# Output columns 1024 to 2047 of w_out as a second panel of seven products

## What is computed

```python
merged = sigmoid(g_a) * (o_a @ w_branch_a) + sigmoid(g_b) * (o_b @ w_branch_b)
h = h + merged @ w_out
hn = rms_norm(h, norm_ffn_g)
h = h + (silu(hn @ w_ffn_gate) * (hn @ w_ffn_up)) @ w_ffn_down
```

## Time and profile before

| | |
|---|---|
| median of the runs | 1259.84 us |
| the profiled execution | 1259.98 us |
| its span | 1258.2 us |
| TensorE busy | 1253.8 us |
| VectorE busy | 1051.5 us |
| ScalarE busy | 757.4 us |
| DMA, mean | 227 GB/s |

### The profile page before, as it was taken

How to read it: one execution, slowest core, us unless ns; L and a number is a source line. 1 busy time by engine, 2 the same in 40 slices (tenths; PEclk the granted TensorE clock), 3 DMA queues, 4 the chain that set the end, 5 groups by cost and what they waited for, 6 DMA issues and landing times.

```text
span 1258.2 us, 14986 instructions
## 1 busy us (share of the span) xinstructions
PE 1253.8 (100%) x5870; PEld 1039.4 (83%) x5870; DVE 1051.5 (84%) x930; ACT 757.4 (60%) x765; POOL 92.1 (7%) x89
## 2 busy tenths in 40 slices
PE   9999999999999999999999999999999999999999
PEld 8888888888878888888888888888888888888887
DVE  6988887677889788779989888878898887888996
ACT  6766665566667555456656665556566555655653
POOL 3312312000000000000000000100000001000000
DMA  9976683855357586955777768976686679866874
GB/s 353 319 253 189 208 262 119 267 162 160 113 190 249 168 296 215 335 166 194 247 247 234 253 184 248 282 249 221 201 263 242 199 216 305 258 221 193 275 220 115
DMA packets 136933, 285.98 MB, mean 227 GB/s; under 512 B 5264, under 2 KB 11936, under 8 KB 133280
## 3 DMA queue, kind: packets, MB, share of 16 engines
q1 hardware_dynamic: 129904, 252.23, 57.0%
q0 software_dynamic: 6784, 32.53, 13.8%
q10 hardware_dynamic: 176, 0.26, 0.1%
HBM read 251.43 MB, written 8.41 MB: 207 GB/s over the span
## 4 chain that ended last, share of the span: by engine, by line
PE 99%; DMA 0%; DVE 0%; SPq 0%; ACT 0%; issue 0%
PE bank L2361 27%; PE bank L2366 27%; PE bank L2362 27%; PE bank L2304 4%; PE bank L2312 4%; PE bank L2305 4%; PE bank L2243 1%; PE bank L2256 1%; PE bank L2517 1%; PE bank L2272 1%; PE bank L2225 0%; DMA raw<-in_w_in 0%; PE bank L2274 0%; PE bank L2530 0%; PE bank L2215 0%; DVE w_lo L1544 0%
## 5 line engine op out<-in xcount | busy, mean ns | idle before, releaser
L1806 DVE TENSOR_TENSOR u_lo<-quad,u_hi 128x2048 fp32r<-128x2048 f32 x245 | 556.5, 2287 | 109.5 <-ACT u_hi L1233 60.1
L1233 ACT ACTIVATE u_hi<-quad 128x2048 fp32r<-128x2048 f32 x250 | 475.4, 1915 | 282.6 <-PE bank L2366 160.9
L2361 PE MATMUL bank<-u_hi,xT_hi 128*128 128x512 f32 x676 | 263.3, 389 | 0.0
L2362 PE MATMUL bank<-u_hi,xT_lo 128*128 128x512 f32 x676 | 263.0, 389 | 0.0
L2366 PE MATMUL bank<-u_lo,xT_hi 128*128 128x512 f32 x740 | 198.1, 389 | 0.0
L2366 PEld LDWEIGHTS bank<-u_lo,xT_hi 128*128 128x128 f32 x740 | 138.7, 188 | 29.2 <-DVE u_lo L1806 0.5
L2362 PEld LDWEIGHTS bank<-u_hi,xT_lo 128*128 128x128 f32 x676 | 126.9, 188 | 26.2
L2361 PEld LDWEIGHTS bank<-u_hi,xT_hi 128*128 128x128 f32 x676 | 126.9, 188 | 26.2
L1544 DVE TENSOR_TENSOR w_lo<-raw,w_hi 128x1024 fp32r<-128x1024 f32 (+1 forms) x64 | 73.3, 1155 | 33.7 <-ACT w_hi L1039 32.1
L2362 PE MATMUL bank<-u_hi,fT_lo 128*128 128x512 f32 (+1 forms) x236 | 90.7, 385 | 0.0
L2361 PE MATMUL bank<-u_hi,fT_hi 128*128 128x512 f32 (+1 forms) x236 | 90.7, 385 | 0.0
(11 more groups left out here) (271 smaller groups left out, 1852.0 us busy)
## 6 DMA issues: line engine op xcount, KB each, us to landing
quad<-in_w_ffn_gate SPq DMA_DIRECT2D x44, 1024.0 KB, 6.8
quad<-in_w_ffn_up SPq DMA_DIRECT2D x44, 1024.0 KB, 6.0
quad<-in_w_ffn_down SPq DMA_DIRECT2D x44, 1024.0 KB, 6.2
quad<-in_w_in SPq DMA_DIRECT2D x41, 1024.0 KB, 6.8
quad<-quad POOLq DMA_DIRECT2D x24, 1024.0 KB, 8.4
raw<-in_w_in SPq DMA_DIRECT2D x16, 1024.0 KB, 5.7
quad<-in_w_out SPq DMA_DIRECT2D x16, 1024.0 KB, 5.2
raw<-in_w_branch_b SPq DMA_DIRECT2D x8, 1024.0 KB, 9.3
```

The costliest lines, as they stand in the source:

```text
L1233: A(st.hi[u.hi][:], st.quad[slot][:], ACT.Copy).then_inc(hi_ready, u.step)
L1806: V.tensor_tensor(st.lo[u.lo][:], st.quad[u.panel.slot[u.raw]][:], st.hi[u.hi][:].bitcast(F32), ALU.subtract).then_inc(lo_ready, u.step)
L2361: M(sums, a_hi(k), hi[:, w], start=start and k == 0, stop=False, skip_group_check=True)
L2362: M(sums, a_lo(k), hi[:, w], start=False, stop=False, skip_group_check=True)
```

## The change

Columns 1024 to 2047 of w_out become a second panel `outs[1]` in the order `ORDER`; U and O units are gone. Units N2 and N3 of a w_out panel are placed in the panel behind it. `panels[0]` has the order `FFN_FIRST_ORDER`. The early units are M1 and M5 of `outs[0]`; the P of `outs[0]` is made by POOL's accumulating DMA, and Z of `outs[0]` is moved from behind N1 to behind M2. The additions to h are single (one half, one token block), and steps of h are placed anew between the units. The load of x goes out one load earlier in SP's queue and still waits for the last merge. (Core of the diff; removed runs of lines, which stand above, are left out.)

```diff
-H_AFTER = 6
-OUT_ORDER = ("M1", "U0", "M5", "M6", "M2", "M7", "N0", "M3", "N1", "M4", "N2", "N3", "U1", "U2", "U3")
+H_AFTER = 5
+OUT_ORDER = ("M1", "M5", "M6", "M2", "M7", "N0", "M3", "N1", "M4")
+FFN_FIRST_ORDER = ("M1", "N2-", "M5", "N3-", "M6", "M2", "M7", "N0", "M3", "M4", "N1")
 FIRST_ORDER = ("O0", "O1", "M1", "O2", "M5", "O3", "M6", "M2", "M7", "N0", "M3", "N1", "M4")
 ORDER = ("M1", "N2-", "M5", "N3-", "M6", "M2", "M7", "N0", "M3", "N1", "M4")
...
+def plan_outs(kt, n, first_index):
+    panels = []
+    index = first_index
+    for col, names in enumerate((OUT_ORDER, ORDER)):
+        p = Panel(n + col, "out2", col, kt, panels[-1] if panels else None)
+        p.i = -1
+        p.add_products()
+        panels.append(p)
+        for name in names:
+            u = (p.prev if name[-1] == "-" else p).unit[name[0:2]]
+            u.index = index
+            p.order.append(u)
+            index += 1
+    return panels
...
+    early = [outs[0].unit["M1"], outs[0].unit["M5"]]
...
+        out_stage = Stage(quad, quad_landed, f_stage.hi, f_stage.lo, ms_hi, ms_lo, m21[:])
+        for panel in outs:
+            panel.stage = out_stage
...
+            steps = 3 * panel.n + {"P": 1, "R": 2, "Z": 3}[name]
+            return steps - (panel.n >= outs[0].n)
+        def p_ready(panel):
+            return (p_summed, 16) if panel is outs[0] else (sum_ready, sums(panel, "P"))
...
+            def sum_p(panel):
+                st = panel.stage
+                pool.wait_ge(st.landed[panel.slot["12"]], panel.landed["12"])
+                pool.wait_ge(early_lo_ready, 1)
+                pool.dma_start(st.quad[panel.slot["11"]][:], st.quad[panel.slot["12"]][:],
+                               accum_op=ALU.add).then_inc(p_summed, 16)
...
-            sum_q(outs)
+            sum_p(outs[0])
+            sum_q(outs[0])
+            sum_q(outs[1])
...
-                    if j in jobs[-3:-1] and k == 3:
-                        early_unit_hi(jobs[-3:-1].index(j))
+                    if (j, k) in ((jobs[-3], 3), (last_bb, 2)):
+                        early_unit_hi(j is last_bb)
...
+            def outs_unit(panel, u):
+                if u.name == "M6" and panel is outs[1]:
+                    copy_m1(panel)
                 if u.name == "M7":
-                    copy_m5(outs)
+                    copy_m5(panel)
                 if u not in early:
                     unit_hi(u)
...
+                if u.name == "M6" and panel is outs[0]:
+                    copy_m1(panel)
+                if panel is outs[0]:
+                    if u.name == "N0":
+                        turned_to_hi(last_bb, mT_hi, last_bb.n)
+                else:
+                    if u.name == "N2":
+                        squares_of(0)
+                    if u.name == "M2":
+                        scaled_to_hi(0)
+                        A(x21, by_group(staged[:, 1, :]), ACT.Copy).then_inc(x21_ready, 1)
+                    if u.name == "M3":
+                        squares_of(1)
+                    if u.name == "M4":
+                        scaled_to_hi(1)
+            def first_unit(panel, u):
                 if u.name == "M6":
                     copy_m1(panel)
                 if u.name == "M7":
                     copy_m5(panel)
                 unit_hi(u)
-                if u.name == "O0":
-                    squares_of(1)
-                if u.name == "O1":
-                    scaled_to_hi(1)
-                if u.name == "M1":
+                if u.name == "N2":
                     x_forms_of_h()
                     squares_of(NB - 2)
-                if u.name == "M6":
+                if u.name == "M2":
                     scaled_to_hi(NB - 2)
-                if u.name == "N0":
+                if u.name == "M3":
                     squares_of(NB - 1)
-                if u.name == "M3":
+                if u.name == "N1":
                     scaled_to_hi(NB - 1)
...
+            def add_to_h(panel, half, t):
+                n = 2 * panel.col + half
+                sums = ((a_bank, b_bank), (c_bank, e_bank))[half][t](panel)
+                if t:
+                    dve.wait_ge(piece_used, (panel.b_done, panel.c_done)[half] + 1)
+                else:
+                    dve.wait_ge((a_summed, c_summed)[half], rows_before(panel) + 1)
+                V.tensor_tensor(h[:, t, columns_of(n)], sums[:], h[:, t, columns_of(n)],
+                                ALU.add).then_inc((h_top_ready, h_ready)[t], 1)
...
-                    if j in jobs[-3:-1] and k == 3:
-                        early_unit_lo(jobs[-3:-1].index(j))
+                    if j in (jobs[-3], last_bb) and k == 3:
+                        early_unit_lo(j is last_bb)
                     if j.prev is not None:
                         follow(j.prev, k, j.pieces)
-                    if j is last_bb and k == 3:
-                        sum_p(outs)
                     a = att_step(j, k, SPLIT_SLOTS - 1)
...
+            def outs_unit(panel, u):
+                before = panel.prev
+                if panel is outs[0]:
+                    if u.name == "M7":
+                        seed_c(panel)
+                    if u.name == "M3":
+                        seed_e(panel)
+                    if u not in early:
+                        unit_lo(u)
+                    if u.name == "M5":
+                        sum_r(panel)
+                        gate_bb(last_bb)
+                    if u.name == "M2":
+                        sum_z(panel)
+                    if u.name == "M7":
+                        merge(last_bb)
+                    if u.name == "M3":
+                        turned_to_lo(mT_hi, mT_lo, last_bb.n, last_bb.n, mT_ready)
+                else:
+                    if u.name == "M1":
+                        dve.wait_ge(h_landed, 16)
+                        add_to_h(before, 0, 0)
+                    if u.name == "M7":
+                        seed_c(panel)
                     unit_lo(u)
...
+                    if u.name == "N2":
+                        add_to_h(before, 0, 1)
+                        sum_p(panel)
+                    if u.name == "N3":
+                        sum_r(panel)
+                        scale_h(0, H_SETS + 1)
+                    if u.name == "M2":
+                        sum_z(panel)
+                    if u.name == "N0":
+                        seed_e(panel)
+                        add_to_h(before, 1, 0)
+                        add_to_h(before, 1, 1)
+                        scaled_to_lo(0)
+                        x_forms_begun()
+                    if u.name == "N1":
+                        scale_h(1, H_SETS + 2)
+                    if u.name == "M4":
+                        scaled_to_lo(1)
+                        x_forms_of_h()
+            def first_unit(panel, u):
+                before = panel.prev
                 if u.name == "M1":
...
+                    add_to_h(before, 0, 0)
                 if u.name == "M7":
                     seed_c(panel)
+                if u.name == "M4":
+                    scale_h(NB - 1, SETS)
+                if u.name == "N1":
+                    scaled_to_lo(NB - 1)
+                unit_lo(u)
+                if u.name == "N2":
+                    add_to_h(before, 0, 1)
+                    sum_p(panel)
+                    x_forms_of_h_lo()
+                if u.name == "N3":
+                    sum_r(panel)
+                    scale_h(NB - 2, SETS - 1)
+                if u.name == "M2":
+                    sum_z(panel)
+                    scaled_to_lo(NB - 2)
                 if u.name == "N0":
-                    scale_h(NB - 1, SETS)
+                    seed_e(panel)
+                    add_to_h(before, 1, 0)
+                    add_to_h(before, 1, 1)
+                if u.name == "N1":
                     dve.wait_ge(h_ss_ready, T * NB)
                     V.tensor_reduce(h_sum[:], h_ss[:], AX.X, ALU.add).then_inc(h_sum_ready, 1)
...
-                        if k == j.pieces - 1:
+                        if k == j.pieces - 1 and j is not last_bb:
                             pe.wait_ge(mT_ready, T * (j.prev.n + 1))
...
                 if u.name == "M1":
-                    pe.wait_ge(branch_b_gated, T * 2)
+                    if before is None:
+                        pe.wait_ge(branch_b_gated, T * 2)
+                    else:
+                        pe.wait_ge(h_top_ready, 2 * before.col + 1)
                     pe.wait_ge(mT_ready, T)
                     ins = product(u, a_bank(panel), *own(panel, 0, 0), True)
                 if u.name == "M5":
-                    pe.wait_ge(branch_b_gated, T * 3)
+                    pe.wait_ge(branch_b_gated, T * (3 + panel.col))
                     pe.wait_ge(ms_ready, 1)
                     ins = product(u, e_bank(panel), *combined(panel, 0), True)
                 if u.name == "M6":
                     pe.wait_ge(m1_copied, panel.n + 1)
...
-            for u in outs.order:
```

(21 more changed lines are left out.)

## The result

The changed kernel takes **1265.86 us**, the median of four runs (1263.95 to 1266.16), beside 1259.76 for the kernel before (four runs): ratio 1.0043, 95% interval 1.0031 to 1.0056. The forecast was 1262.4, its range ended at 1265.0. The sign was right, the size was not: of +6.1 us the forecast had 2.6.

What follows compares the result with a forecast made beforehand. TensorE's list of products was taken as the bound, as long as VectorE and ScalarE deliver in time. -2.72 + 2.0 + 3.2 + 0.1 = +2.6 us gave a forecast of 1262.4 us, range 1258.9 to 1265.0.

Steps and rivals of the forecast that it cites:

- what TensorE saves: From the first w_out unit to the second gate/up panel: 42 products become 41, -2.72 us.
- the first panel: M1 to M7 of the first w_out panel: M7 waits for its seed of c, 2.0 us lost together.
- two small terms: First w_out panel: M7's lo comes late, 0.35 us; the last branch set's turn waits for merge, 0.15 us.
- the path of 73 us: VectorE, N2's hi to M7's lo of panels[0]: 73.0 us against TensorE's 69.9; 3.2 us lost with restarts.
- no wait: Rival, whole stretch: the queues absorb everything, 1257.1 us; chance 0.09.
- only the first one: Rival: only the first panel's wait comes, VectorE makes up its 3 us; 1259.2 up to 1261.3 us; chance 0.22.
- the term of 0.1 behind the stretch: In panels[1], lead falls from 5.4 to 3.9 us; 1.8 were spare at its seed of c: 0.1 us lost.
- Edits at nothing: P by DMA, h's later load, single additions, M4 and N1 exchanged in panels[0], a removed wait: priced at no cost.
- the clock: Rival, over the stretch: new pauses bring the 1.2 GHz level; 5 us of it gives 1265 us; chance 0.03.
- three pauses of 0.5 to 2.2 us: New TensorE pauses in the stretch, named in the clock rival as what the lower clock might follow.
- late data or a lag that repeats: Rival: P by DMA or weights late, or M7 of each following panel short of its seed; 1263.8 to 1267 us; chance 0.12.

Runs made afterwards that it cites:

- e5: e2 with Z of outs[1] and of panels[0] made by POOL's accumulating DMA, not VectorE: 1257.15 us, ratio 0.9977.
- e2: e1 with Z of the first w_out panel moved back behind the seed of e, ahead of M3's lo: 1261.17 us, ratio 1.0007.
- e6: e2 with only order changed in panels[0]: scaled_to_lo(2) behind M7's lo, Z behind the additions at N0: 1258.82 us, ratio 0.9991.
- e1: Changed kernel with VectorE's reduce to h_sum moved from behind N1 of panels[0] to behind M3's lo: 1262.54 us, ratio 1.0021.
- e3: Kernel before with the reduce to h_sum moved from ahead of the seed of e to directly ahead of M3's lo: 1264.7 us, single run.
- e4: Changed kernel with VectorE waiting for h_rs behind the reduce to h_sum, before its next lo: 1264.73 us, ratio 1.0036.
- e7: e5 with the reduce to h_sum moved back behind N1 of panels[0]: 1259.99 us, ratio 1.0001.

## Why the prediction was right or wrong

**Right: what TensorE saves.** 2.72, by e5's 2.76 with nothing in the way.

**Right: the first panel.** The seed of c was forecast at 495.18 and came at 494.98, with the whole stretch 0.22 earlier; the loss 2.0 is 1.9. Its two small terms offset each other: at M7's lo, 0.35 was given (0.29 by the prediction's own rule) and 0.18 came, at the turn 0.15 was given and 0.32 came. e2 shows the cause of the main one: Z ahead of the seed.

**Right: the path of 73 us.** It was priced to lose 3.2 us at two M7; the losses are 0.4 and 2.75. e6 and e5, where order and length of VectorE's queue are changed, take it away in part and whole. The rivals in which no wait or only the first one comes fell by this. M1 of `panels[1]` was due at 604.9, forecast 605.1.

**Check of the whole sum.** e1 is the changed kernel without what I missed. Its seven runs at a mean clock of 1.00 have a median of 1262.28, the forecast is 1262.4. Beside its own measurement of before that is +2.15, where the forecast had +2.6; the term of 0.1 behind the stretch shows in no wait of after or e1.

**Wrong: "Edits at nothing".** There I priced the exchange of M4 and N1 in `panels[0]` as "the gate's first half is then read 2.7 us before M1 needs its bank, and takes 0.7". The step asks when the gate's unit is placed, and not when its other input is there. `first_unit` in the diff also moves the reduce of `h_sum`, from ahead of M3's lo to behind N1, and no sentence of mine follows that. With the durations that `h_rs` had in before, the new place still fits: reduce at 600.94, POOL done by 602.2, ScalarE's hi done at 602.66, gate read by 603.4, M1 due at 604.91, with 1.5 us to spare. What failed beneath the missing sentence is that a duration was taken to hold at another neighbour: in before, POOL's first operation lay under a VectorE operation with an operand in PSUM, and the second could start ahead of the next lo; in after it lies under one with both in SBUF. The measured price is 4.78 of POOL where 0.90 stood, and 2.04 on the path.

This was on show in the trace of before, where the same two lines of POOL's code also make the scales of the attention heads. VectorE's and POOL's timeline of before, for four elements per partition:

```profile
61.71 4.48 DVE L1806 TENSOR_TENSOR u_lo<-quad,u_hi 128x2048 fp32r<-128x2048 f32 x2
61.88 4.36 POOL L960 TENSOR_SCALAR q_ms<-q_ss 128x4 f32<-128x4 f32 x1 [8.81 <-DVE q_ss L1605]
66.33 1.03 POOL L961 TENSOR_TENSOR q_rs<-q_ms,minus_half 128x4 f32<-128x4 f32 x1
```

The first took 4.36 us, until VectorE's two lo were done (61.71 + 4.48 = 66.19), and the second, in VectorE's pause, 1.03. A hold of this length at the new place of the reduce (601.20) would keep `h_rs` back past 606, and M1 with it.

The Trainium skill, "SBUF — State Buffer", section Who interferes with whom, states that a VectorE instruction with two SBUF inputs contends with a GpSimd instruction that reads SBUF; its section Summary: rules for kernel authors adds that the second to issue is blocked until the first finishes. e1, e3, e4 and e6 agree on which pairs collide. On the length they don't: e3's 16.50 us lie over eight VectorE instructions. And VectorE isn't held in return: in before the lo at 587.45 starts under POOL's second operation (587.31 to 588.02) and takes 2.28, and all 245 of these lo take 2.28 to 2.30. Read beside the new place of the reduce, this rule was the one that speaks against the change, and I weighed another.

**Wrong by size: the clock.** I gave it 0.03 and three pauses of 0.5 to 2.2 us as its possible cause. It came: in the profiled execution of after behind the fourth pause, which I hadn't seen, in those of e2 and e4 behind the pause of 2.2, which I had listed. In after one run of four has a mean clock of 1.00 and takes 1263.95; the three at 0.999 take 1265.86 to 1266.16. Over e1, e2 and e7 the medians of runs below 1.00 and at 1.00 lie 1.4, 1.2 and 1.2 us apart. So some 1.2 to 1.9 us in part of the executions is its price; 1.7 in the profiled one of after. The 27 runs of before beside e5 to e7, all of e5 and all of e6, which have no pause over 1.0 us, are at 1.00.

The median of after is then 1262.4 + 2.0 + 1.7, less 0.2 for the earlier start of the profiled stretch: 1265.9. My rival "late data or a lag that repeats" (1263.8 to 1267) has the time that came, but not the cause: no DMA ends a wait in after, and the later panels repeat none.

## What to carry to other kernels

Follow every instruction that a moved step issues, the smallest too, to its last reader: here a reduce of 0.16 us on VectorE decided on some 3 us at the other end of a chain through POOL and ScalarE. A duration holds for its neighbours in the trace; before a GpSimd step is priced at nothing, look for the same operation elsewhere in the trace and at what VectorE does beside it, and leave VectorE a pause or operations with a PSUM operand there. At 93 to 95% (after, e6) a VectorE queue needs its order worked out operation by operation, and relief by a DMA that has room is worth more than reordering (all of the 2.75 us against 1.65 here).

## What the hardware showed that I had not expected

**A tiny POOL operation held for 16.5 us.** 0.18 to 0.19 us beside a pause or operations with an operand in PSUM (before, e1, e2, e4, e5, e6), 2.14 and 2.15 in after and e7, 16.50 in e3. In e6 both of POOL's operations lie wholly under a pair that reads PSUM; VectorE's and POOL's timeline of e6:

```profile
590.82 1.27 DVE L1611 TENSOR_TENSOR staged<-bank,gains_x 128x512 f32<-128x512 f32 x2
591.00 0.18 POOL L972 TENSOR_SCALAR h_ms<-h_sum 128x2 f32<-128x2 f32 x1 [3.48 <-DVE h_sum L2192]
591.27 0.71 POOL L973 TENSOR_TENSOR h_rs<-h_ms,minus_half 128x2 f32<-128x2 f32 x1
```

In after and e7 the first operation ended with the VectorE operation during which it started; in e3 it found no gap between eight, and at 61.88 of before none between two. Why POOL gets in between two of VectorE's in the one case and not in the other stays open; no run tells them apart.

**The clock falls behind single pauses of 1.9 to 2.9 us, in part of the executions.** TensorE's timeline of e2, behind its one wait of 2.17:

```profile
583.96 0.50 PE L2412 MATMUL bank<-u_hi,xs_hi 128*128 128x512 f32 x1
...
584.68 0.63 PE L2412 MATMUL bank<-u_hi,xs_hi 128*128 128x512 f32 x1
```

Up to 583.96 the matmuls start 0.23 apart, from 584.26 to 587.25 they start 0.43 apart. In the profiled executions of e1 and of after the wait of 2.2 at the same unit is followed by none of this; in after the fall comes behind the later wait of 1.9, in e3 behind that of 2.9, and e7's of 1.9 is followed by none. In the executions without a profile only the mean clock shows that it fell, not where. The Trainium skill, "TensorE: Matmul & The Clock Gate", section HAM oscillation, tells of kernels that fall back at each wait for data; here one wait suffices, and not each time. Behind the wait of 1.2 us in the first panel (after, e1, e4) no profile shows a fall.
